# One token block ahead of the other: block 0 goes alone from attention to its first gathered rows, block 1 follows in pieces among them

## The chip, the core and the metric

The kernel runs as one program on one core of a Trainium2 chip. The core has TensorE (PE, matrix products), VectorE (DVE), ScalarE (ACT), GpSimd (POOL) and SyncE (SP), each with its own in-order instruction stream, and sixteen DMA engines that move data between the chip's memory and the core. Streams meet only at semaphores. In this kernel SP issues the weight loads, POOL issues the gathers and some loads, ACT a few. The metric is the device time of one execution in microseconds; the median of three runs of the kernel before is 1559.52 us (1557.63 to 1566.49).

## The reference

The input is 256 tokens of width 1024 in float32, one layer. The first half computes

```python
h = rms_norm(x, attn_norm_g)
q, k, v, qi, ki, wi, glu_in, gates = split(h @ w_in)
y_att = dsa_attention(q, k, v, qi, ki, wi, rel_bias) @ w_att_out   # 64 keys of 256 kept per token by an index score
y_conv = conformer_conv(glu_in, conv_w, ...)                       # depthwise, 31 taps, layer norm, silu, @ w_conv_out
g = sigmoid(gates + b_gate)
x = x + (g[0] * y_att + g[1] * y_conv) @ w_out
h2 = rms_norm(x, ffn_norm_g)
x = x + peer(h2, w_peer_q, sub_keys, expert_u, expert_v)
x = x + sigmoid(rms_norm(x) @ w_ple_gate) * (p @ w_ple_proj)
```

`peer` is the part that matters here. Each token forms 8 heads of two queries (`h2 @ w_peer_q`, 2048 columns), scores each against 128 keys, takes the best 16 of each, the best 16 of their sums, and so picks 128 of 16384 experts. For each pick it takes a row of `expert_u` and one of `expert_v` (1024 numbers each): the dot product of the token with the first, through a gelu and times a softmax gate, weighs the second in the sum. The picks differ per token, so the rows are gathered. The second half is a recurrent layer (a scan in both directions over a context and over the tokens) and a convolutional feed-forward layer; the modulation of its norms comes from the product of two condition vectors with a 1024 by 6144 matrix (`ada_w`), which needs nothing of the first half.

## The kernel before

The 256 tokens are two blocks of 128, one token per partition. Weight matrices come as tiles of up to 512 columns (2 MB) into a ring of two slots: SP (`sp_weights`, L482) issues tile i when tile i-2 has been multiplied, in the order of `weight_tiles`, and two PSUM buffers G alternate in the same way (`pe_tile`, `freed`). A product is taken as features (`pe_features`, L502: weights stationary, 256 tokens as columns) or as tokens (`pe_tokens`, L512: tokens stationary, 512 weight columns); each runs over both blocks. One product of float32 matrices counts as two instructions.

Order on TensorE: `pe_project` (norm, then glu_g, glu_a, q, k, v, qi, kiwi), `pe_attention` (index scores, four gate tiles, the convolution's mean and variance, then logits, turned probabilities and values of block 0 and of block 1), `pe_mix` (conv_out, att_out, mix_out, two tiles each), `pe_queries` (norm and queries). ScalarE runs beside in `act_first` and `act_queries`, VectorE in `dve_first` and `dve_queries`. VectorE's softmax, top keys and convolution stand in that order by hand, and `some(n)` puts n units of the ada products between them (`dve_modulation`, L1135 and L1139). There are 64 units: 16 tiles of 0.5 MB are used twice and 32 once. POOL loads these 48 tiles into four slots (L1119), each when the tile four before it is used, and its later gathers stand behind the loads in its stream.

The selection (`dve_select`) works on a quarter of the heads of one block at a time. `spread_e` and `spread_g` place picks and gates over the partitions through TensorE (L1189). POOL's `pool_rows` (L1475) then issues 256 gathers, one pick of 128 tokens each: 128 rows of 8 KB, 1.05 MB, into a ring of eight. A gather waits for its quarter's picks and for the use of the row eight before it. A group is two rows: VectorE's dot products (L1490), ScalarE's gelu and diagonal (L1496 to L1506), TensorE's sum (L1521). Block 0 has groups 0 to 63, block 1 has 64 to 127.

Other work is cut into pieces that run between the groups. `run_order` lets TensorE run piece k behind group k, and VectorE and ScalarE one group later. In `beside` stand the other seven selections (ten pieces each, one begins every eight groups), the last query tile (five pieces), the context's norm and projections (from piece 10), the scan over the context, and the ple projection: 126 places of 128 groups. Behind the last group come ple, the scan over the tokens and the feed-forward layer.

## Time and profile before

| | us |
|---|---|
| median of 3 runs | 1559.52 |
| lowest, highest run | 1557.63, 1566.49 |
| profiled execution: span from first to last instruction | 1554.9 |
| the runs' median less that span | 4.6 |
| first gathered row issued | 318.26 |
| last gathered row issued | 974.97 |

The trace is of one execution and times are counted from its first instruction. Its own time is known as that span; the runs were timed apart from it, and their median is 4.6 us longer. In rows of the trace "busy" of an engine is the time in which it executed something; the DMA share is the mean busy share of the sixteen DMA engines; the granted clock is a share of TensorE's full speed. "<-" behind an idle time names what ended it. Matrix products are pipelined, so that merged rows overlap by a tenth or two of a microsecond.

### The profile page before, as it was taken

To read this page: it belongs to the slowest core of one execution; us is meant where nothing else is said; L and a number is where in the kernel's file an instruction comes from. 1 tells how busy PE (TensorE), PEld (TensorE's weight loads), DVE (VectorE), ACT (ScalarE), POOL (GpSimd) and SP (SyncE) were. 2 spreads that over 40 slices of the span, in tenths; PEclk is the share of its full clock that TensorE was granted. 3 is DMA by queue.
4 is the path that set the end of the run, shared out by engine and by line. 5 is a ranking of instruction groups with operands and counts; after the bars stand their busy time and mean duration, and the time that the engine had idled before them with its cause. 6 is when DMAs were issued, how large, how long until landed. Compare 5 with 4: busy or idle time off the path is not lost.

```text
span 1554.9 us, 26679 instructions
## 1 busy us (share of the span) xinstructions
PE 1212.9 (78%) x11282; PEld 834.9 (54%) x11282; DVE 926.5 (60%) x2067; ACT 431.5 (28%) x1094; POOL 347.1 (22%) x315
## 2 busy tenths in 40 slices
PE   7989898894385533457856775799987888999998
PEld 6467784772153100125524452468877774888843
DVE  2887666657797988785677655321455343455512
ACT  2111420132432422543364332423243211110100
POOL 1000012034354555454455544000000000000000
PEclk9997999996597855569878996899999999999999
DMA  9551459699999999999999999624300023344432
GB/s 381 195 191 66 144 205 390 238 383 419 414 410 420 420 422 421 421 414 419 416 421 420 420 418 418 240 82 163 109 9 3 4 111 108 122 163 161 137 140 104
DMA packets 109720, 409.73 MB, mean 264 GB/s; under 512 B 8456, under 2 KB 33552, under 8 KB 76448
## 3 DMA queue, kind: packets, MB, share of 16 engines
q0 software_dynamic: 44576, 297.35, 46.5%
q1 hardware_dynamic: 63552, 106.48, 19.2%
q10 hardware_dynamic: 1472, 4.20, 1.0%
q8 instruction: 88, 1.44, 0.4%
q14 instruction: 32, 0.26, 0.0%
HBM read 405.89 MB, written 2.11 MB: 262 GB/s over the span
## 4 chain that ended last, share of the span: by engine, by line
PE 58%; DMA 22%; DVE 10%; ACT 4%; issue 3%; POOL 2%; another core or an unknown queue 0%; POOLq 0%; DVEq 0%; ACTq 0%; SPq 0%
PE psum L502 20%; DMA arena<-in_experts,arena 17%; PE psum L1942 8%; PE psum L2454 5%; PE psum L512 4%; DVE arena L1490 4%; PE psum L1521 3%; DMA arena<-in_lora_up 2%; PE psum L755 2%; PE psum L1269 2%; POOL arena L1475 2%; PE psum L2244 2%; PE psum L760 2%; DMA arena<-in_ada_wT 2%; PE psum L741 2%
## 5 line engine op out<-in xcount | busy, mean ns | idle before, releaser
L1475 POOL DMA_INDIRECT arena<-in_experts,arena x256 | 317.1, 1239 | 383.2 <-PE psum L1521 299.8
L1521 PE MATMUL psum<-arena 128*32 128x512 f32 x1024 | 185.4, 805 | 238.2 <-ACT arena L1506 231.6
L502 PE MATMUL psum<-actT,weights 128*128 128x256 f32 x1312 | 287.3, 381 | 0.0
L502 PEld LDWEIGHTS psum<-actT,weights 128*128 128x128 f32 x1312 | 250.3, 191 | 35.7 <-issue 1.5
L1521 PEld LDWEIGHTS psum<-arena 128*32 128x32 f32 x1024 | 22.7, 121 | 329.5 <-ACT arena L1506 307.3
L1490 DVE CUSTOM_DVE_ANT_0 arena<-arena 128x1024 f32<-128x1024 f32 x96 | 116.7, 1224 | 50.9 <-DMA arena<-in_experts,arena 50.1
L1490 DVE CUSTOM_DVE_ANT_0 arena<-weights,arena 128x1024 f32<-128x1024 f32 x96 | 116.6, 1223 | 37.1 <-DMA arena<-in_experts,arena 35.1
L1496 ACT ACTIVATE arena<-arena 128x2 f32<-128x2 f32 x128 | 26.1, 204 | 364.3 <-DVE arena L1490 350.4
L1942 PE MATMUL psum<-arena 64*64 64x64 f32 (+1 forms) x2816 | 89.7, 231 | 17.4 <-DVE arena L2059 7.1
L1942 PEld LDWEIGHTS psum<-arena 64*64 64x64 f32 x2816 | 84.1, 142 | 26.0 <-issue 14.6
L1490 DVE CUSTOM_DVE_ANT_0 arena<-normed,arena 128x1024 f32<-128x1024 f32 x64 | 77.2, 1225 | 22.1 <-DMA arena<-in_experts,arena 20.3
L1119 POOL DMA_DIRECT2D arena<-in_ada_wT x48 | 25.5, 531 | 229.7 <-DVE mod L1135 229.7
L2454 PE MATMUL psum<-weights,arena 128*128 128x512 f32 x176 | 75.7, 592 | 0.0
L512 PE MATMUL psum<-weights,actT 128*128 128x512 f32 x160 | 69.2, 592 | 0.0
L1506 ACT ACTIVATE arena<-const,arena 128x32 f32<-128x32 f32 x256 | 66.3, 306 | 0.0
L1501 ACT ACTIVATE arena<-arena 128x1 f32<-128x1 f32 x256 | 61.5, 287 | 12.1 <-ACT arena L1496 0.4
L2528 DVE SCALAR_TENSOR_TENSOR arena<-arena,small 128x256 f32<-128x256 f32 x154 | 61.9, 478 | 0.0
L2454 PEld LDWEIGHTS psum<-weights,arena 128*128 128x128 f32 x176 | 33.4, 190 | 41.7 <-issue 41.6
L1942 PEld LDWEIGHTS psum<-actT,arena 64*64 64x64 f32 x1152 | 39.3, 134 | 21.4 <-ACT arena L2027 12.0
L512 PEld LDWEIGHTS psum<-weights,actT 128*128 128x128 f32 x160 | 30.4, 190 | 37.8 <-issue 37.8
L1942 PE MATMUL psum<-actT,arena 64*64 64x64 f32 x1152 | 45.5, 221 | 5.7 <-issue 4.3
L675 ACT ACTIVATE normed<-xres 128x512 f32<-128x512 f32 (+1 forms) x13 | 9.0, 692 | 146.4 <-DVE xres L2544 60.3
(390 smaller groups left out, 1897.0 us busy)
## 6 DMA issues: line engine op xcount, KB each, us to landing
weights<-in_w_in SPq DMA_DIRECT2D x18, 2048.0 KB
arena<-in_ada_wT POOLq DMA_DIRECT2D x48, 512.0 KB, 6.3
weights<-in_ffn_w_up SPq DMA_DIRECT2D x22, 1024.0 KB
weights<-in_ffn_w_down SPq DMA_DIRECT2D x5, 2048.0 KB
weights<-in_w_out SPq DMA_DIRECT2D x4, 2048.0 KB
weights<-in_w_peer_q SPq DMA_DIRECT2D x4, 2048.0 KB
arena<-in_experts,arena POOLq DMA_INDIRECT x256
weights<-in_w_ple_gate SPq DMA_DIRECT2D x2, 2048.0 KB
```

What stands on the lines that cost most here:

```text
L502: mm = nc.tensor.matmul(out[:, c * T:(c + 1) * T], w[:, k, c * P:(c + 1) * P], act[:, k, :], start=(k == 0), stop=(k == kc - 1))
L512: mm = nc.tensor.matmul(out[:, b * 512:(b + 1) * 512], act[:, k, b * P:(b + 1) * P], w[:, k, :], start=(k == 0), stop=(k == kc - 1))
L741: mm = nc.tensor.matmul(chunk_bank(c)[:, b * P:(b + 1) * P], xres[:, b, c * P:(c + 1) * P], norm_diag[:, b, :], start=True, stop=True)
L755: mm = nc.tensor.matmul(out[:, 2 * i * T:(2 * i + 1) * T], w[:, k, 2 * i * P:(2 * i + 1) * P], actT[:, k, :], start=(k == 0), stop=(k == D ...
L1475: nc.gpsimd.indirect_dma_start(out=rows[:, n % RING, :], out_offset=None, in_=dram["experts"], in_offset=bass.IndirectOffsetOnAxis(ap=eidx ...
L1490: ins = nc.vector.tensor_tensor_reduce(rows[:, pos, 0:D], quad_row(b, k % QUADS), rows[:, pos, 0:D], 1.0, 0.0, ALU.mult, ALU.add, dots[:, ...
L1501: nc.scalar.activation(acts[:, g, j:j + 1], gelu[:, g, j:j + 1], ACT.Copy, scale=gate[:, b, bass.ds(t * RING + (g * GROUP + j), 1)]).then_ ...
L1506: nc.scalar.activation(diag[:, pos, :], K("ident_q"), ACT.Copy, scale=acts[:, g, j:j + 1]).then_inc(S("diag_ok"), 1)
L1521: mm = nc.tensor.matmul(SUMS[sum_part(k, i), i, :], diag[:, pos, :], rows[:, pos, D + 512 * i:D + 512 * (i + 1)], start=first, stop=last, ...
L1942: mm = nc.tensor.matmul(dst[half[c], g, at + q * n:at + (q + 1) * n], left(g, c, q), right(g, c, q), start=True, stop=True)
L2454: return nc.tensor.matmul(aux[2 * b + n], ffT[:, f, b * P:(b + 1) * P], w[:, k, 512 * n:512 * (n + 1)], start=(f == 0), stop=(f == FC - 1))
L2528: st.run(nc.vector.scalar_tensor_tensor(dst, src, w, dst, ALU.mult, ALU.add))
```

## The change

Block 0 is taken through attention, mixing, norm and two of four query tiles by itself. Block 1's attention runs between; its mixing, norm and queries become 19 pieces (`pe_follow`, `act_follow`, `dve_follow`) among the groups 0 to 18, and query tiles 2 and 3, which serve both blocks, lie among them. Tiles `att_out`, `mix_out` and `peer_q0`, `peer_q1` are loaded once per block. Products for one block have 128 columns (`pe_block_features`), or one group of 128 tokens (`pe_block_tokens`). The norm has tags n2a and n2b, one per block, each with a square of two halves, a root, a diagonal and turned chunks of 128 columns; each block's normed rows are written out apart.

In `dve_first` the ada units are spread as 16, 2, 6, 9, 11, 6, 3, then 5 ahead of the selection, and the last 6 behind it; VectorE mixes block 1's attention between the indices and the gates of the first selection. POOL fetches the condition vectors at its start, the keys and the norm's gain behind ada tile 8, and holds row 5 until all ada tiles are used, since rows 5 to 7 of the ring lie where the ada tiles were. The arena is laid out anew for this; scores go through G instead of a bank of their own. The selections begin at pieces 2, 11, 19 and so on, the context's work at piece 21 instead of 10, and the free place behind each pair of the scan is taken out.

```diff
-    for i in range(4):
+    def gate_tile(i):
         tile(f"gate{i}", part(w, 0, DC, GATE0 + 512 * i, 512))
+    def conv_tile(i):
+        tile(f"conv_out{i}", part(dram["w_conv_out"], 0, CC, 512 * i, 512))
+    gate_tile(2)
+    gate_tile(3)
+    conv_tile(0)
+    gate_tile(0)
+    gate_tile(1)
+    conv_tile(1)
+    for b in range(TB):
+        for i in range(2):
+            tile(f"att_out{i}_{b}", part(dram["w_att_out"], 0, CC, 512 * i, 512))
+        for i in range(2):
+            tile(f"mix_out{i}_{b}", part(dram["w_out"], 0, DC, 512 * i, 512))
+        if b == 0:
+            for i in range(2):
+                tile(f"peer_q{i}", part(dram["w_peer_q"], 0, DC, 512 * i, 512))
+    for i in (2, 3):
+        tile(f"peer_q{i}", part(dram["w_peer_q"], 0, DC, 512 * i, 512))
     for i in range(2):
-        tile(f"conv_out{i}", part(dram["w_conv_out"], 0, CC, 512 * i, 512))
-    for i in range(2):
-        tile(f"att_out{i}", part(dram["w_att_out"], 0, CC, 512 * i, 512))
-    for i in range(2):
-        tile(f"mix_out{i}", part(dram["w_out"], 0, DC, 512 * i, 512))
-    for i in range(4):
-        tile(f"peer_q{i}", part(dram["w_peer_q"], 0, DC, 512 * i, 512))
+        tile(f"peer_q{i}_1", part(dram["w_peer_q"], 0, DC, 512 * i, 512))
...
+        def pe_block_features(pe, name, src, chunks_of=4):
+            w, out = pe_tile(pe, name)
+            kc = w.shape[1]
+            for c in range(4):
+                for k in range(kc):
+                    mm = nc.tensor.matmul(out[:, c * P:(c + 1) * P], w[:, k, c * P:(c + 1) * P], src[:, k, :],
+                                          start=(k == 0), stop=(k == kc - 1))
+                if c == 3:
+                    mm.then_inc(S("tile_done"), 1)
+                if (c + 1) % chunks_of == 0:
+                    yield
+        def pe_block_tokens(pe, name, src, chunks_of=DC):
+            w, out = pe_tile(pe, name)
+            for k in range(DC):
+                mm = nc.tensor.matmul(out[:, 0:512], src[:, k, :], w[:, k, :], start=(k == 0), stop=(k == DC - 1))
+                if k == DC - 1:
+                    mm.then_inc(S("tile_done"), 1)
+                if (k + 1) % chunks_of == 0:
+                    yield
...
+            pe_index(0)
+            pe.wait_ge(S("rel_in"), 64)
+            pe.wait_ge(S("ix_relu"), 1)
+            for i in range(4):
+                mm = nc.tensor.matmul(aux[i], K("flip"), toepf[:, 512 * i:512 * (i + 1)], start=True, stop=True)
+            mm.then_inc(S("toep_pe"), 1)
+            pe_features(pe, "gate2", actT)
+            pe.wait_ge(S("toep_cp"), 1)
+            pe_logits(0)
+            pe_features(pe, "gate3", actT)
+            pe_probs_turned(pe, 0)
+            pe.wait_ge(S("cvT_ok"), CC)
+            pe_features(pe, "conv_out0", cvT)
+            pe_values_of(pe, 0)
             pe_features(pe, "gate0", actT)
+            pe.wait_ge(S("av_cp"), 1)
+            pe_index(1)
+            pe_features(pe, "gate1", actT)
             pe.wait_ge(S("ix_relu"), 2)
+            pe_logits(1)
+            pe_features(pe, "conv_out1", cvT)
+            for i in range(2):
+                all_of(pe_block_features(pe, f"att_out{i}_0", attT[0]))
+            pe.wait_ge(S("mix_ok"), 2)
+            all_of(pe_block_tokens(pe, "mix_out0_0", mixT[0]))
+            pe_probs_turned(pe, 1)
+            all_of(pe_block_tokens(pe, "mix_out1_0", mixT[0]))
+            pe_values_of(pe, 1)
...
+            top_keys(0)
+            some(6)
+            softmax_first(0)
+            softmax_last(0)
+            some(9)
             st.settle()
+            conv_mixed(0)
+            some(11)
+            top_keys(1)
+            softmax_first(1)
+            conv_mixed(1)
             for i in range(2):
+                st.settle()
+                dve_att_mixed(dve, 0, i)
+            softmax_last(1)
+            some(6)
+            dve_mix_add(dve, 0, 0)
+            some(3)
+            dve_mix_add(dve, 0, 1)
...
+        def dve_att_mixed(dve, b, i):
+            tile_, dst = f"att_out{i}_{b}", mixT[b][:, 4 * i:4 * i + 4, :]
+            tmp = (late_tmp if b else first_tmp)[:, i, :].rearrange("p (c t) -> p c t", c=4)
+            wait_freed(dve, f"gate{i}")
+            wait_freed(dve, f"conv_out{i}")
+            nc.vector.tensor_tensor(tmp, product(dve, tile_)[:, 0:512].rearrange("p (c t) -> p c t", c=4),
+                                    gatt[b][:, 4 * i:4 * i + 4, :], ALU.mult).then_inc(freed(tile_), 1)
+            wait_freed(dve, tile_)
+            nc.vector.tensor_tensor(dst, dst, tmp, ALU.add).then_inc(S("mix_ok"), 1)
+        def dve_mix_add(dve, b, i):
+            dst = halves_of(xres, b, i)
+            nc.vector.tensor_tensor(dst, product(dve, f"mix_out{i}_{b}")[:, 0:512], dst, ALU.add).then_inc(
+                freed(f"mix_out{i}_{b}"), 1)
...
             pool.dma_start(relb, dram["rel_bias"]).then_inc(S("rel_in"), 16)
             pool.dma_start(onehot, dram["onehot"]).then_inc(S("rel_in"), 16)
+            pool.dma_start(silu_c.rearrange("p n k -> p (n k)"), dram["cc"].partition_broadcast(P)).then_inc(S("c_in"), 16)
             pool.wait_ge(S("rel_cp"), 1)
             pool.dma_start(scratch, hbias).then_inc(S("rel_in"), 16)
             pool.wait_ge(S("rel_in"), 48)
             overlap = bass.AP(scratch.tensor, 0, [[1, P], [3 * P, AH], [1, T]])
             pool.dma_start(toepf.rearrange("p (s t) -> p s t", s=AH), overlap).then_inc(S("rel_in"), 16)
-            pool.dma_start(keysT, dram["keysT"]).then_inc(S("keys_in"), 16)
-            pool.dma_start(gbc, dram["ffn_norm_g"].partition_broadcast(P)).then_inc(S("gbc_in"), 16)
-            pool.wait_ge(S("chunk_pe"), DC)
-            pool.dma_start(silu_c.rearrange("p n k -> p (n k)"), dram["cc"].partition_broadcast(P)).then_inc(S("c_in"), 16)
             for j in range(6 * DC):
                 if j >= ADA_SLOTS:
                     pool.wait_ge(S("ada_used"), j - ADA_SLOTS + 1)
                 pool.dma_start(adaw[:, j % ADA_SLOTS, :], dram["ada_wT"][j * P:(j + 1) * P, :]).then_inc(
                     S(f"ada_in{j % ADA_SLOTS}"), 16)
+                if j == 2 * ADA_SLOTS:
+                    pool.dma_start(keysT, dram["keysT"]).then_inc(S("keys_in"), 16)
+                    pool.dma_start(gbc, dram["ffn_norm_g"].partition_broadcast(P)).then_inc(S("gbc_in"), 16)
         def dve_modulation(dve, st):
...
         def pe_queries(pe):
-            pe_norm_tile(pe, "n2", "peer_q0")
+            pe_norm_query(pe, 0, "peer_q0")
             pe.wait_ge(S("keys_in"), 16)
-            for i in range(QUARTERS - 2):
-                if i:
-                    pe_features(pe, f"peer_q{i}", actT)
-                pe_scores(pe, i)
+            pe_scores(pe, 0)
+            all_of(pe_block_features(pe, "peer_q1", actT[:, :, 0:P]))
+            pe_scores(pe, 1)
+            pe.wait_ge(S("av_cp"), TB)
+            for i in range(2):
+                all_of(pe_block_features(pe, f"att_out{i}_1", attT[1]))
             pe_spread(pe, "e", 0, FIRST["e"])
...
+            pe_spread(pe, "g", 0, FIRST["g"])
...
+        FOLLOW_PIECES = 19
+        def pe_follow(pe):
+            pe.wait_ge(S("mix_ok"), 4)
+            for i in range(2):
+                for _ in pe_block_tokens(pe, f"mix_out{i}_1", mixT[1], DC // 2):
+                    yield
+            yield
+            for c in range(DC):
+                pe_block_chunk(pe, 1, c)
+            yield
+            for k in range(DC):
+                chunk_copied(pe, BLOCK_NORM[1], k)
+            for _ in pe_features_by_chunk(pe, "peer_q2", actT):
                 yield
-            pe_scores(pe, QUARTERS - 1)
+            for c in pe_features_by_chunk(pe, "peer_q3", actT):
+                if c == 0:
+                    pe_scores(pe, 2)
+                yield
+            for n in (4, 5):
+                for c, _ in enumerate(pe_block_features(pe, QUERY_TILES[n][0], actT[:, :, P:2 * P], 2)):
+                    if c == 0:
+                        pe_scores(pe, n - 1)
+                    yield
+            pe_scores(pe, 5)
+            yield
...
+        def dve_follow(dve, st):
+            yield
+            dve_mix_add(dve, 1, 0)
+            yield
+            yield
+            dve_mix_add(dve, 1, 1)
+            dve_block_diagonal(dve, 1)
+            yield
+            yield
+            copy_block_chunks(dve, 1, 1)
+            yield
+            dve_block_row(dve, 1)
             yield
...
         def dve_queries(dve, st, mod):
+            dve_block_diagonal(dve, 0)
+            copy_block_chunks(dve, 0, 1)
+            dve.wait_ge(S("chunk_pe"), chunks_before("n2a") + DC)
+            dve.wait_ge(S("silu_c"), 2)
+            dve_block_row(dve, 0)
+            for _ in range(MODS_BEFORE_SELECT):
+                next(mod, None)
+            select = dve_select(dve, st, 0, 0)
+            for _ in range(7):
+                next(select)
+            for i in range(2):
+                dve_att_mixed(dve, 1, i)
+            all_of(select)
             for _ in mod:
                 pass
             dve.wait_ge(S("ada_used"), 6 * DC)
...
                     g, j = divmod(k, GROUP)
                     pool.wait_ge(S("row_used"), rows_ahead(former[0], t, g) + j + 1)
+                if n == 5:
+                    pool.wait_ge(S("ada_used"), 6 * DC)
                 nc.gpsimd.indirect_dma_start(
...
         def sp_ctx(sp):
-            wait_freed(sp, "mix_out1")
+            sp.wait_ge(S("mix_ok"), 4)
             act_load(sp, "lora", loraup, dram["lora_up"].rearrange("d p n -> p d n"))
             sp.wait_ge(S("sc_pe"), QUARTERS * TB)
+            sp.wait_ge(S("normed_out"), 32)
             act_load(sp, "ctx", ctok, dram["ctx"].rearrange("(b p) d -> p b d", p=P))
...
                 for j in range(TB):
-                    yield one(pe_pair, act_pair, dve_pair, 3 + SOLVE_LEVELS, d, j, rest=1)
+                    yield one(pe_pair, act_pair, dve_pair, 3 + SOLVE_LEVELS, d, j)
             yield one(pe_chain, None, dve_chain, NCH, rest=2)
-        SPREAD_BEFORE = 2
+        SPREAD_BEFORE = 3
         n_first = len(beside)
-        pieces = [[] for _ in range(SELECT_EVERY * (n_first - 1) + SELECT_PIECES)]
+        begins = [2] + [11 + SELECT_EVERY * i for i in range(n_first - 1)]
+        pieces = [[] for _ in range(begins[-1] + SELECT_PIECES)]
         for i, f in enumerate(beside):
             for k in range(f["pieces"]):
-                pieces[SELECT_EVERY * i + k].append((i, k))
+                pieces[begins[i] + k].append((i, k))
         early = [dict(act=act_ctx_norm, dve=dve_ctx_norm, pieces=1),
                  dict(pe=pe_ctx_in, act=act_ctx_in, dve=dve_ctx_in, pieces=17)]
         scan = list(scan_stages(ctx_m, "c"))
         early.append(scan.pop(0))
         early.append(dict(pe=pe_quads, act=act_quads, pieces=QUADS))
-        turn = SELECT_EVERY * (SPREAD_BEFORE - 2) + SELECT_PIECES
+        turn = begins[SPREAD_BEFORE - 2] + SELECT_PIECES
         for f in early:
             for k in range(f["pieces"]):
                 pieces[turn].append((len(beside), k))
                 turn += 1
             beside.append(f)
         assert turn <= len(pieces)
-        for k in range(QUARTERS + 1):
+        for k in range(FOLLOW_PIECES):
             pieces[k].append((len(beside), k))
-        beside.append(dict(pe=pe_late_queries, act=act_late_queries, pieces=QUARTERS + 1))
+        beside.append(dict(pe=pe_follow, act=act_follow, dve=dve_follow, pieces=FOLLOW_PIECES))
         n_first = len(beside)
         beside += scan
```

## Rows read from the trace of the kernel before

**Rows 1.** Page: the span in 40 slices; DMA busy tenths, then GB/s.

```profile
DMA  9551459699999999999999999624300023344432
GB/s 381 195 191 66 144 205 390 238 383 419 414 410 420 420 422 421 421 414 419 416 421 420 420 418 418 240 82 163 109 9 3 4 111 108 122 163 161 137 140 104
```

**Rows 2.** Windows: stretch, busy of PE, PEld, DVE, ACT, POOL; clock, DMA share, GB/s.

```profile
0.00:318.30 318.30, 281.86 (x1197) 212.93 (x1198) 214.34 (x459) 60.95 (x85) 30.04 (x60) 0.95 0.63 226
318.00:975.00 657.00, 400.48 (x4588) 211.93 (x4587) 486.40 (x1187) 249.97 (x784) 315.23 (x256) 0.75 1.01 418
990.00:1555.00 565.00, 521.51 (x5440) 405.36 (x5432) 218.44 (x410) 113.30 (x207) 0.00 (x0) 0.98 0.30 105
```

**Rows 3.** Timeline of POOL: start us, duration us, line, operation, idle before it.

```profile
318.26 1.01 POOL L1475 DMA_INDIRECT arena<-in_experts,arena  x1 [41.65 <-DVE arena L1444]
...
974.97 1.94 POOL L1475 DMA_INDIRECT arena<-in_experts,arena  x1 [0.30 <-issue]
```

**Rows 4.** Timeline of TensorE: first start, time of the merged instructions, count.

```profile
98.75 3.62 PE L802 MATMUL psum<-actT,weights 128*128 128x256 f32 x16
...
146.37 1.89 PE L837 MATMUL psum<-arena,const 128*128 128x256 f32 x8
...
148.09 13.98 PE L502 MATMUL psum<-actT,weights 128*128 128x256 f32 x64
...
165.52 1.71 PE L873 MATMUL psum<-arena 64*128 64x128 f32 x16 [1.72 <-ACT arena L943]
...
183.80 1.58 PE L864 MATMUL psum<-arena 128*64 128x128 f32 x16 [1.69 <-ACT arena L956]
...
186.05 2.96 PE L873 MATMUL psum<-arena 64*128 64x256 f32 x16 [0.68 <-ACT arena L959]
...
202.94 1.97 PE L856 MATMUL psum<-const,arena 128*128 128x128 f32 x16
...
231.46 7.17 PE L502 MATMUL psum<-arena,weights 128*128 128x256 f32 x32 [0.35 <-DMA weights<-in_w_att_out]
...
242.34 29.40 PE L512 MATMUL psum<-weights,arena 128*128 128x512 f32 x64 [3.70 <-issue]
...
278.28 2.95 PE L741 MATMUL psum<-normed,xres 128*128 128x128 f32 x12 [6.54 <-DVE normed L722]
...
298.53 2.02 PE L1260 MATMUL psum<-arena 128*128 128x128 f32 x16 [1.19 <-ACT arena L1311]
```

**Rows 5.** DMA issues by line: transfer, queue, KB of one, median us to landing.

```profile
xres<-in_x SPq DMA_DIRECT2D x1, 1024.0 KB, 5.1
```

**Rows 6.** Timeline of VectorE: the end of a softmax, and two ada units in a row.

```profile
200.60 2.29 DVE L1057 TENSOR_TENSOR arena<-arena 128x2048 f32<-128x2048 f32 x1
...
233.74 1.23 DVE L1135 CUSTOM_DVE_ANT_0 arena<-arena 128x1024 f32<-128x1024 f32 x1
...
234.89 1.22 DVE L1135 CUSTOM_DVE_ANT_0 arena<-arena 128x1024 f32<-128x1024 f32 x1
```

**Rows 7.** The line that loads the ada tiles: us from issue to landing.

```profile
DMA to landing us min/median/max: 3.7/6.3/13.2
```

**Rows 8.** Waits by line: us in total, times, longest us.

```profile
DVE arena L1135 <- DMA arena<-in_ada_wT: 11.2, 12, 2.2
```

**Rows 9.** Window of the norm and the interleaved half of the first query tile.

```profile
278.28:290.50 12.22, 12.22 (x66) 11.37 (x67) 4.43 (x8) 1.90 (x4) 0.00 (x0) 0.88 0.45 177
```

**Rows 10.** Timeline of VectorE: start and end of the first selection.

```profile
300.44 0.87 DVE L1374 MAX8 arena<-arena 128x8 f32<-128x128 f32 x4 [4.34 <-ACT arena L1316]
...
317.79 0.19 DVE L1444 CAST arena<-psum 128x32 uint32<-128x32 f32 x1 [1.31 <-PE psum L1189]
```

**Rows 11.** Chain of waits, start us and us; then the window of the first.

```profile
356.95 32.78 DMA arena<-in_lora_up
389.81 11.80 DMA arena<-in_ctx
...
356.90:389.80 32.90, 11.67 (x80) 3.32 (x72) 24.51 (x71) 9.94 (x31) 14.74 (x12) 0.59 1.02 420
```

More of the change, by code:

```diff
@@ L799, in pe_project @@
             pe_features(pe, "qi", actT)
+            pe.wait_ge(S("cv_dve"), 1)
+            for c in range(CC):
+                mm = nc.tensor.matmul(AUX[:, 0, 0:T], K("conv_mean"), ycv[:, c, :], start=(c == 0), stop=(c == CC - 1))
+            mm.then_inc(S("cv_pe"), 1)
             w, out = pe_tile(pe, "kiwi")
@@ L809, in pe_attention @@
         def pe_attention(pe):
[L811 to L814 removed]
             pe.wait_ge(S("qk_n"), 1)
[L817 removed]
+            pe.wait_ge(S("cv_dve"), 2)
             for g in range(4):
```

582 lines of the change are left out of this document (341 added, 241 removed).

## The prediction

> **What bounds the kernel now.** The page's slices come first [rows 1]: the sixteen DMA engines are full (share 9, about 420 GB/s) for seventeen slices, and half idle in the eight before. The windows give the sizes [rows 2]: up to 318.3 us they run at 0.63 and 226 GB/s, from 318 to 975 us at 1.01 and 418 GB/s, while TensorE has 400 of 657 us busy and VectorE 486. POOL's queue names the two ends [rows 3]: the first gathered row is issued at 318.26 us, the last at 974.97. So the kernel is three stretches in series: 318 us of dependent work before the first row, 657 us bounded by bytes (256 rows of 1.05 MB are 268 of some 275 MB), and 565 us behind (990 to 1555), which the change leaves alone. An earlier first row is worth its whole advance, but each byte added behind it costs 1/418 us per kB, that is 2.5 us per 1.05 MB, whatever hides its arithmetic.
>
> **The change, part by part.** *The path to the first row.* I walk it from 98.9 us, the end of the qi tile, which nothing moves on TensorE: ten more ada units before the convolution fill VectorE's idle time there, since the condition vector is fetched at POOL's start; if they end 3 us late, TensorE still has tile kiwi to hide it. Prices from [rows 4]; a tile of 64 instructions is 14.0, one of 32 is 7.2.
> - Convolution mean (1.9), kiwi (two halves of 3.6), 16 transposes (2.0), variance (1.9), index products of block 0 (1.7), their ReLU on ScalarE (1.0), flip (eight instructions of 512 columns, 0.46 each as in the mixing tile, 3.7): 98.9 to 118.3. The old wait of TensorE between 109 and 131 us mostly goes.
> - gate2, gate3 and logits (14.0+14.0+1.7) cover top keys and softmax of block 0 on VectorE; turned probabilities 1.0, conv_out0 7.2, values 1.6, gate0 14.0, index products of block 1 (3.0), gate1 14.0, logits 3.0, conv_out1 7.2: 199.0.
> - Output tiles of one block have 128 columns instead of 256. At 128 columns 16 instructions take 2.02, so 0.126 each; 32 per tile are 4.0. The first ends at 203. The second's 1 MB is issued when conv_out1 ends; 1 MB lands in 5.1 [rows 5], so it runs from about 205 to 209, and VectorE's two products and sums (1.4) end at 210.4.
> - Mixing: a token tile of one block is a quarter of the 29.40 shown for 64 instructions, 7.35. Its 2 MB (about 10 by twice 5.1) is issued at 203: it runs 213 to 220, then 16 transposes 2.0, the second mixing tile to 230.
> - VectorE has the end of block 1's softmax (two passes of 2.29 and a reciprocal [rows 6]) to 215.2, then nine ada units. Four are loaded, one every 1.15 [rows 6]. The others wait for loads: 6.3 us from issue [rows 7], then 2.0 apart (1.15, and 11.2/12 of waiting as in the old row [rows 8]). That gives 231.9, so the addition (half of a pass of 1024, 0.7) ends at 232.6: VectorE, not TensorE, is late here. Square, root, reciprocal and diagonal (0.8+0.3+0.5 and handovers): 234.5.
> - Norm and first query for one block: the interleaved half took 12.2 [rows 9] for both blocks. Half its columns, but a chain of copies that doesn't halve: 8.1 (6 to 12 possible). The remaining half of the tile 4.0. Two copies, scores and copy 2.6: 249.2. VectorE meanwhile owes five ada units, the last loaded late: 251.8.
> - Selection from the first maximum to the indices took 300.44 to 317.98, 17.5 [rows 10]: 269.3. TensorE has its first spread ready only just in time: query 1 (64 of 0.126, 8.1), its scores, and block 1's att_out (twice 4.0, the second's weights landing about 262) end near 267. The first row isn't free yet: POOL issues in order, and the load of ada tile 47 stands before the rows and waits for tile 43. VectorE first mixes block 1 (3.0), ends the selection's gates (2.0) and uses tiles 42 and 43 (2.3); POOL's issue 0.5. **First row at 277**, against 318.3: a gain of 41. Ends: 262 if the ada loads are never late and handovers cost nothing beyond the rows, 292 if each of some forty handovers costs 0.4 more.
>
> Narrow matmuls ahead of the first row: 128 instructions (two att_out tiles and the first query tile of 64). At 0.126 us [rows 4] they cost little more than half of a 256-column one (14.0/64, 0.219). The Trainium skill (TensorE: Matmul & The Clock Gate, Back-to-back issue gap) speaks against this: spacing is set by weight load and matmul together, with about 81 ns at 128 columns and 131 at 512. By that ratio one would take 0.28 here (0.62 of 29.40/64), and the 128 would cost 20 us more than by the row.
>
> *What stands behind the first row.* New inside the byte-bound stretch: query tiles 2, 0 again and 1 again (6.3 MB), the rest of tile 3, which was partly loaded before 318 (1.4), two ada tiles (1.05) and block 1's normed rows (0.5): 9.3 MB at 418 GB/s is 22. The second set of att_out and mix_out lands by about 277 (mix_out is issued at 262 and 267). Ends 18 (all weights for pieces come a tile earlier) and 27 (both mix tiles inside).
>
> POOL's new wait at row 5 for all ada tiles holds every later row, and with them all four engines. Tiles 46 and 47 are issued at 277, land by 283.5 (13.2 at the worst), and are used by 286. Rows 0 to 4 and the two tiles are 6.3 MB, 15 us of transfers, so the DMA has work to 292: nothing, at worst 4.
>
> *The pieces.* TensorE gets 19 pieces of at most 6 us among groups that the DMA brings every 5; old pieces of the same kind did not lower the DMA share. Their weights are the risk. In the old run 2.6 MB of weights took 32.78 us beside gathers [rows 11], 80 GB/s, a fifth. Up to the context's norm (piece 21) the weight queue must bring six tiles, lora and context, 14.2 MB: 177 us at that rate, from about 293. The 46 rows that go with it are 48 MB, 142 us at the other 340 GB/s. So TensorE, and VectorE at the context's norm, will wait for weights with groups queued behind. The ring's eight rows (20 us) go on meanwhile; once it is empty, weights have all engines to themselves and catch up. What is lost is each restart: a group's products (1.1), POOL's issue (1.0) and the first landing, about 3.5. I count two: 7. Ends 0 and 32 (rival 2). A gain is excluded, since the stretch already runs at 1.01.
>
> *At nothing:* block 1's additions, copies and row on VectorE (about 5 us; it has 170 idle in the stretch), the removed rests between scan pairs (125 pieces instead of 126, of 128 groups), the spread banks and the arena's new layout. If the scan no longer fitted before the last group, its remainder would show behind the rows, a few us.
>
> **Sum.** Profiled span 1554.9 - 41 + 22 + 7 = 1542.9. The runs' median 1559.52 is 4.6 above that span, so **1547**.
>
> **Rivals.**
> 1. *The ada loads are not in the way.* For it: until VectorE's last block-0 softmax they have long pauses to run ahead. Against: four slots, and the old kernel stood on them twelve times. First row at 262, 24 of bytes (mix_out not landed), 3 of restarts: -29, **1531**.
> 2. *Slower: the weight queue stays at 80 GB/s even when the rows pause.* Then 177 us of weights set the 23 groups that by bytes take 62 MB/418 = 149, and the ring idles for the rest: about 32 instead of 7, net +13, **1572**. It decides once weights get under some 95 GB/s (14.2 MB in 149 us). For it: the 32.78. Against: 1 MB landed in 5.1 with little beside it.
> 3. *A late first row:* TensorE's handovers, or a lower clock after waits, bring it to 295. Then -23 + 21 + 7, **1564**: the bytes eat the advance, no change.
> 4. *Narrow matmuls spaced by their weight loads:* twelve of 128 columns took 2.95 just after a wait, 0.246 each [rows 4]. At that price the 128 cost 15 more: **1562**. The skill's rule above says the same in kind.
>
> **How the numbers follow.** Forecast 0.50 (own range 1536 to 1558), rival 1 0.18, rival 2 0.12, rival 3 0.16, rival 4 0.04. What a measurement tells from no change is 0.5%, 7.8 us. The forecast's case gives faster 0.40 and same 0.10; rival 1 faster 0.18; rivals 3 and 4 same 0.17 and slower 0.03; rival 2 slower 0.12. Range 1522 to 1573, which takes in rival 2's price and a first row at 262 without restarts.
>
> **What would show it.** POOL's first gather near 277, released by VectorE's use of an ada tile, not by the indices; first-row advance minus rows' end advance near 29; weights in the chain of waits among groups 6 to 22, and a dip of the DMA share at two places there; the last 565 us the same. Wrong if the row stretch grows by under 15 or over 45 us, or if the first gather is past 292.

## The result

The changed kernel takes 1590.2 us (median of four runs, 1585.9 to 1592.0), the kernel before 1558.6 beside it: a ratio of 1.0195, 95% interval 1.0165 to 1.0225. It is slower by 31 us, where 1547 was forecast, and outside the range. The profiled run took 1591.4, its span 1589.6, 34.7 more than before.

The page's slices [rows 1] and the windows [rows 2] of the changed kernel:

```profile
DMA  9643958899996999999999999724300032444442
GB/s 353 231 133 122 341 180 305 278 421 421 418 405 239 419 420 421 421 420 414 419 420 421 419 418 420 312 80 159 106 9 3 4 109 71 154 149 143 141 152 105
```

```profile
0.00:307.36 307.36, 257.26 (x1202) 199.75 (x1202) 207.35 (x453) 58.94 (x90) 29.93 (x60) 0.93 0.68 240
307.36:1003.95 696.59, 427.04 (x4790) 239.49 (x4791) 495.40 (x1204) 254.07 (x791) 314.56 (x256) 0.77 0.99 406
480.00:500.00 20.00, 5.30 (x24) 1.97 (x24) 11.71 (x50) 8.28 (x18) 2.73 (x2) 0.50 0.27 89
```

A thirteenth slice of 239 GB/s is new: a hole in the stretch that was full before. POOL's timeline gives the two ends [rows 3], and the hole from POOL's side:

```profile
307.36 2.04 POOL L1771 DMA_INDIRECT arena<-in_experts,arena  x1 [0.31 <-issue]
...
465.31 0.93 POOL L1771 DMA_INDIRECT arena<-in_experts,arena  x1 [0.30 <-issue]
496.31 1.79 POOL L1771 DMA_INDIRECT arena<-in_experts,arena  x1 [30.06 <-PE psum L1817]
...
1003.95 0.93 POOL L1771 DMA_INDIRECT arena<-in_experts,arena  x1 [0.30 <-issue]
```

The first row is 10.9 earlier, not 41; the last is 29.0 later; from it to the end there are 585.6 us, before 579.9. So -10.9 + 39.9 + 5.7 = +34.7, the spans' difference.

**A ledger of the DMA.** GB/s times length gives the bytes of a window; bytes over 420 GB/s, the rate of the full stretches, give the time that they need; what is left of the time is "not full", whether the engines were idle or busy at a lower rate. Before, [rows 2] give 71.9 MB up to 318.3 and 274.6 to 975: 346.5 MB, 825 us, 150 not full (147 of them ahead of the first row). After: 73.8 + 282.8 = 356.6 MB, 849 us, 155 not full (132 ahead of the first row, 23 among the rows). The 10.1 MB more are 24 us. The time that is not full, which the change would have had to cut, even grew by 5.

**Where the first row lost 30 us.** TensorE's timeline of the changed kernel, and the walk in the prediction beside it: tile qi (84.9 before, 95.7 now), gate2 (118.3 forecast, 131.5), gate0 waits for its weights, the first att_out tile of block 0 (199.0 forecast, 217.3).

```profile
52.63 43.20 PE L551 MATMUL psum<-weights,actT 128*128 128x512 f32 x96 [6.09 <-DMA weights<-in_w_in]
95.66 13.98 PE L541 MATMUL psum<-actT,weights 128*128 128x256 f32 x64
...
131.49 13.98 PE L541 MATMUL psum<-actT,weights 128*128 128x256 f32 x64
...
174.78 15.77 PE L541 MATMUL psum<-actT,weights 128*128 128x256 f32 x64 [4.37 <-DMA weights<-in_w_in]
...
217.29 3.73 PE L935 MATMUL psum<-arena,weights 128*128 128x128 f32 x32
```

The line of tile qi in the kernel before, and the line that loads the ada tiles up to 60 us, before and after:

```profile
84.93 13.98 PE L502 MATMUL psum<-actT,weights 128*128 128x256 f32 x64
...
arena<-in_ada_wT POOLq DMA_DIRECT2D x7, 512.0 KB, 10.3
...
arena<-in_ada_wT POOLq DMA_DIRECT2D x12, 512.0 KB, 10.7
```

VectorE begins the selection at 269.7 (251.8 forecast) and has the picks at 285.7, and then waits for the spread, as its timeline shows; the chain of waits has the cause, the second att_out tile of block 1:

```profile
269.73 0.87 DVE L1668 MAX8 arena<-arena 128x8 f32<-128x128 f32 x4
...
285.45 0.29 DVE L1734 TENSOR_TENSOR arena<-arena,const 128x128 f32<-128x128 f32 x1
299.46 0.19 DVE L1738 CAST arena<-psum 128x32 uint32<-128x32 f32 x1 [13.71 <-PE psum L1410]
```

```profile
275.81 17.87 DMA weights<-in_w_att_out
293.68 0.04 issue
293.73 5.47 PE psum L935 x32
299.19 0.24 PE psum L1410 x8
```

So the 30 are 10.7 at tile qi, 7 more up to the selection, 12.5 at the spread. These are times of one execution; a3 below shows that another can differ by 7.7 here.

**The hole.** The chain of the rows' stretch [rows 11] holds the lora load and, begun only when it has landed, the context:

```profile
342.18 43.00 DMA weights<-in_w_peer_q
...
404.82 28.48 DMA weights<-in_w_peer_q
...
445.70 35.16 DMA arena<-in_lora_up
480.95 5.52 DMA arena<-in_ctx
```

The 35.16 are not the price of lora's 0.5 MB. SP had issued `ctx_v`, a weight tile of 2.1 MB, 0.4 us ahead of it on the same queue; that tile took 29.5 to land, and lora landed 6 behind it. The two are 2.6 MB in 35.2 us, 74 GB/s, near the 80 of the kernel before [rows 11]:

```profile
445.29 0.37 SPq L521 DMA_DIRECT2D weights<-in_w_in  x1
445.70 0.60 SPq L588 DMA_DIRECT2D arena<-in_lora_up  x1
...
weights<-in_w_in SPq DMA_DIRECT2D x1, 2048.0 KB, 29.5
```

The groups behind the context's norm stand until 486.5, POOL has issued its eight rows by 466, and when the last of them has landed there is next to nothing to move (share 0.27 from 480 to 500).

### The profile page after: what moved, and what is told of

It is laid out like the page before. It is cut to its first block, busy times and chain, and to the rows that moved or that the text cites. A ratio compares the mean times of both kernels' runs of the same rounds, so it can differ in the third digit from the quotient of the medians.

```text
span 1589.6 us, 27114 instructions
## 1 busy us (share of the span) xinstructions
PE 1213.9 (76%) x11474; PEld 847.8 (53%) x11474; DVE 928.6 (58%) x2076; ACT 433.8 (27%) x1112; POOL 345.4 (22%) x315
## 4 chain that ended last, share of the span: by engine, by line
PE 53%; DMA 32%; DVE 7%; ACT 4%; issue 3%; POOL 2%; SPq 0%; POOLq 0%; DVEq 0%; ACTq 0%
DMA arena<-in_experts,arena 19%; PE psum L541 17%; DMA weights<-in_w_peer_q 6%; PE psum L2239 5%; PE psum L551 5%; PE psum L2751 5%; PE psum L1817 3%; DVE arena L1786 3%; DMA weights<-in_w_in 3%; DMA arena<-in_lora_up 2%; PE psum L2541 2%; PE psum L935 2%; POOL arena L1771 2%; PE psum L947 2%; PE psum L801 1%
## 5 line engine op out<-in xcount | busy, mean ns | idle before, releaser
L1817 PE MATMUL psum<-arena 128*32 128x512 f32 x1024 | 176.5, 769 | 228.1 <-ACT arena L1802 228.0
L541 PE MATMUL psum<-actT,weights 128*128 128x256 f32 x1248 | 273.1, 381 | 4.4 <-DMA weights<-in_w_in 4.4
L541 PEld LDWEIGHTS psum<-actT,weights 128*128 128x128 f32 x1248 | 237.9, 191 | 38.5 <-DMA weights<-in_w_in 4.6
L2239 PE MATMUL psum<-arena 64*64 64x64 f32 (+1 forms) x2816 | 82.5, 223 | 17.7 <-DVE arena L2356 7.1
L2239 PEld LDWEIGHTS psum<-arena 64*64 64x64 f32 x2816 | 78.3, 135 | 24.3 <-issue 11.1
L1797 ACT ACTIVATE arena<-arena 128x1 f32<-128x1 f32 x256 | 61.4, 287 | 12.4 <-ACT arena L1792 0.7
L2825 DVE SCALAR_TENSOR_TENSOR arena<-arena,small 128x256 f32<-128x256 f32 x154 | 61.9, 480 | 0.0
L1200 DVE SCALAR_TENSOR_TENSOR arena<-arena,small 128x256 f32<-128x256 f32 x120 | 47.6, 482 | 0.0
L2239 PEld LDWEIGHTS psum<-arena,actT 64*64 64x64 f32 x896 | 39.6, 156 | 12.4 <-issue 4.5
```

What stands on the lines that cost most here:

```text
L541: mm = nc.tensor.matmul(out[:, c * T:(c + 1) * T], w[:, k, c * P:(c + 1) * P], act[:, k, :], start=(k == 0), stop=(k == kc - 1))
L1200: st.run(nc.vector.scalar_tensor_tensor(ycv[:, c, :], src, w, ycv[:, c, :], ALU.mult, ALU.add))
L1797: nc.scalar.activation(acts[:, g, j:j + 1], gelu[:, g, j:j + 1], ACT.Copy, scale=gate[:, b, bass.ds(t * RING + (g * GROUP + j), 1)]).then_ ...
L1817: mm = nc.tensor.matmul(SUMS[sum_part(k, i), i, :], diag[:, pos, :], rows[:, pos, D + 512 * i:D + 512 * (i + 1)], start=first, stop=last, ...
L2239: mm = nc.tensor.matmul(dst[half[c], g, at + q * n:at + (q + 1) * n], left(g, c, q), right(g, c, q), start=True, stop=True)
L2825: st.run(nc.vector.scalar_tensor_tensor(dst, src, w, dst, ALU.mult, ALU.add))
```

## The experiments

Times are medians of 5 to 12 runs; the ratio is to the kernel before, run between them on the same chip (1558.4 to 1559.0). a1 to a4 each alter the changed kernel in one place.

**a1_spread_first.**

```diff
+            pe_spread(pe, "e", 0, FIRST["e"])
             for i in range(2):
                 all_of(pe_block_features(pe, f"att_out{i}_1", attT[1]))
-            pe_spread(pe, "e", 0, FIRST["e"])
...
+            for _ in range(2):
+                next(mod, None)
             for i in range(2):
                 dve_att_mixed(dve, 1, i)
```

> TensorE spreads the first picks ahead of block 1's two att_out tiles, and VectorE does two of its last ada units ahead of mixing block 1, so that POOL's last two ada loads no longer stand behind them. All expectations are against the changed kernel (1590.2 us; first gather 307.4, context landed 486.5, DMA share 0.27 from 480 to 500). Both theories: first gather near 291. Theory A (an earlier first row is worth its advance less the bytes that then fall behind it; some 3.5 MB, 8 us): 1582. Theory B (the weights' order sets the row stretch: the context still lands near 486, whenever rows begin): the hole before it grows by about as much as the first row gains, 1590 within 3.

1581.7, ratio 1.0146 (1.0122 to 1.0169). First gather 286.79, 20.6 earlier; last gather 996.58, 7.4 earlier; the DMA share from 480 to 500 is 0.42, from 460 to 480 it is 0.82. Theory A's number, though the context also came earlier (issued 471.5, not 481).

**a2_quads_late.** It moves the quad tokens: eight loads, issued by ScalarE, that bring block 0's normed tokens back from the chip's memory, 256 KB into 32 partitions each.

```diff
-            for half in range(2):
-                act_quad_tokens(act, half)
             act_query(act, 1)
             act_scores(act, 1)
             for _ in act_select(act, 0, 0):
                 pass
+            for half in range(2):
+                act_quad_tokens(act, half)
```

> ScalarE issues block 0's eight quad-token loads behind the first selection instead of ahead of query 1. If the second att_out tile of block 1 landed late (17.9 us for 1 MB, DMA share 1.0 at 240 to 270 GB/s) because of these loads, it lands about 284 instead of 293.7, the first gather is near 297, and every later weight starts 10 us earlier: 1580 by theory A and by theory B. Rival (the wait is due to the ada and row-out traffic, or the tile is only issued too late): first gather within 3 of 307, time within 3 of 1590.

1580.7, ratio 1.0141 (1.0112 to 1.0171), as expected. In the chain the second att_out tile of block 1 now takes little more than half as long:

```profile
271.48 9.55 DMA weights<-in_w_att_out
```

First gather 294.35. The loads ahead of the selection were the cause of that wait: this 1 MB took 17.0 to 18.8 in the five runs with the quad tokens there (the changed kernel, a1, a3, a4, b3) and 5.5 to 9.6 in the nine that load all of it with the quad tokens later.

**a3_ctx_first.**

```diff
-        ACT_LOADS = ("lora", "ctx", "pT", "gup", "fg")
+        ACT_LOADS = ("ctx", "lora", "pT", "gup", "fg")
...
+                if name == "ctx_v":
+                    sp_ctx(sp)
                 if name == "ctx_lora":
-                    sp_ctx(sp)
+                    sp.wait_ge(S("mix_ok"), 4)
+                    act_load(sp, "lora", loraup, dram["lora_up"].rearrange("d p n -> p d n"))
...
         def sp_ctx(sp):
-            sp.wait_ge(S("mix_ok"), 4)
-            act_load(sp, "lora", loraup, dram["lora_up"].rearrange("d p n -> p d n"))
```

> SP issues the context ahead of ctx_v and of the lora load, which it stood behind. Theory A and B alike, if this order alone makes the hole: context landed near 460 instead of 486.5, no hole at 480 to 500 (DMA share 0.27 before), 13 to 15 us less: 1576. Rival (the hole is only moved, since ctx_v, 2 MB, now comes 1 MB later and TensorE waits for it with groups queued behind): 1586 to 1590, and a wait for ctx_v's weights in place of the context's.

1569.8, ratio 1.0076 (1.0054 to 1.0098): 1.2% of 1559 less than the changed kernel, 19 us, where 14 was expected. The context landed at 453.2. The window that was a hole is full:

```profile
0.00:299.67 299.67, 251.87 (x1202) 194.35 (x1202) 207.50 (x453) 59.06 (x90) 30.07 (x60) 0.95 0.69 246
299.67:981.63 681.96, 430.31 (x4792) 240.41 (x4792) 495.59 (x1204) 254.89 (x796) 318.12 (x255) 0.77 1.01 416
480.00:500.00 20.00, 16.90 (x92) 10.40 (x93) 16.87 (x51) 4.42 (x20) 8.95 (x8) 0.81 1.02 421
```

Not full among the rows: 6.5 us, 23 before the edit. The edit takes the context ahead of two loads, `ctx_v` and lora; which of them made the wait was not tried apart, but by the landings above it was mostly `ctx_v`. Up to 440 us this program is the changed kernel's; that its first gather is at 299.67 shows how far one execution differs from another there (7.7).

**a4_ada_later.** `some(16)` and `some(2)` become `some(6)` and `some(12)`.

> Ten ada units go back from ahead of the convolution to behind it (6 and 12 instead of 16 and 2), so that their loads and the keys' stand no longer beside the weights of tiles glu to q. Theory (the ada loads held up the weights, 6.1 us at tile q and 2 to 3 ahead of it): tile qi begins near 86 instead of 95.7, the first gather is 8 to 10 earlier, and so is the end: 1581. Rival (VectorE is late after the convolution and takes the same 10 us there: ten units of 1.15): qi near 86, but the first gather within 3 of 307 and the time within 3 of 1590.

1587.0, ratio 1.0181 (1.0159 to 1.0204), not told apart from the changed kernel's. TensorE's timeline has tile qi 10 earlier, and the gain given back at the transposes, which wait for VectorE:

```profile
85.67 13.98 PE L541 MATMUL psum<-actT,weights 128*128 128x256 f32 x64
...
116.43 3.30 PE L992 MATMUL psum<-const,arena 128*128 128x128 f32 x16 [8.14 <-DVE arena L1214]
```

The first gather is at 302.63, 4.7 earlier, and the time 3.2 less: a little past the rival's 3 us on both, but within what executions differ by, and far from the theory's 1581. So the rival holds: ten units cost about as much behind the convolution as their loads cost ahead of it.

**b1_three** has the edits of a1, a2 and a3. **b2_earlier** has them too, with the two ada units behind `dve_block_diagonal(dve, 0)`, and `some(10)`, `some(8)`.

> The three edits that gained by themselves, in one kernel: picks spread ahead of block 1's att_out, quad tokens behind the selection, context ahead of ctx_v and lora. Theory A (an earlier first row is worth its advance less the bytes that then fall behind it): first gather near 284 (it was 299.7 with the context's edit alone, 1569.8), last gather 7 to 9 earlier than there, so 1561. If the three gains of 8.5, 9.5 and 20 simply add: 1552. Theory B (the weight queue sets the stretch): the row stretch is as long again as the first row is early, a new hole (DMA share under 0.9 in some 20 us) at the context or the query tiles, 1568 to 1570.

> As b1_three, but the two ada units stand in VectorE's wait behind block 0's diagonal, so that POOL's last ada loads are out before the indices, and the units ahead of and behind the convolution are 10 and 8 (16 and 2 before). Theory A: first gather 5 to 8 earlier than in b1_three, near 277; each us of it worth about half after the bytes: 3 to 4 less than b1_three. Theory B: the same time as b1_three within 2.

1564.2, ratio 1.0041 (1.0018 to 1.0064), and 1564.4, ratio 1.0038 (1.0023 to 1.0052). b2's windows:

```profile
0.00:282.13 282.13, 245.19 (x1133) 187.58 (x1134) 202.21 (x441) 59.00 (x90) 29.93 (x60) 0.95 0.69 248
282.13:976.98 694.85, 440.13 (x4861) 250.38 (x4861) 499.62 (x1212) 254.09 (x791) 316.30 (x255) 0.78 1.01 413
```

The first gathers are at 286.61 and 282.13, 13 and 17.5 ahead of a3's, the last at 980.82 and 976.98, only 0.8 and 4.7 ahead. By the ledger a3 and b2 move the same bytes (357 MB); b2 has 3.3 MB more of them behind its first row. Neither theory gave 1564 for both.

**b3_fewer_bytes**, on a3; **b4_before_ctx_first**, a3's edit made in the kernel before.

```diff
+                    few = 1 if name in ("peer_q0_1", "peer_q1_1") else kc
-                    sp.dma_start(dst[:, :, at:at + n], view).then_inc(S(f"landed{i % WSLOTS}"), 16)
+                    sp.dma_start(dst[:, 0:few, at:at + n], view[:, 0:few, :]).then_inc(S(f"landed{i % WSLOTS}"), 16)
```

> The context's edit (1569.8), and of the second loads of query tiles 0 and 1 only the first of eight chunks is loaded, 3.67 MB less; the products run at full length on what the slots held, so the second block's picks differ. If bytes alone set the row stretch at 418 GB/s: 8.8 less, 1561. If TensorE's waits for these tiles hold groups up besides: 14 or more less, 1556 or under. If other work sets the pace there: 1567 or more.

> The kernel before with the context's load ahead of ctx_v and lora. If the hole belongs to the changed kernel alone (in the kernel before VectorE waited 4.5 us for the context, and the DMA share stayed at 1.0): 1559 within 3. If a late context cost the kernel before too: 5 or more less, 1554 or under.

b3: 1559.6, ratio 1.0013 (0.9999 to 1.0027), 10.2 less than a3 for 3.67 MB: 2.8 us per MB, where the full rate gives 2.4, near the forecast for bytes alone. b4: 1558.5, ratio 0.9999 (0.9988 to 1.0011): the hole is the changed kernel's own.

**c1_free_bytes** is b2 with `few` for all six second loads. **c2_spaced** is b2 with more groups for a piece's weights:

```diff
-        FOLLOW_PIECES = 19
+        FOLLOW_PIECES = 21
...
-                for c, _ in enumerate(pe_block_features(pe, QUERY_TILES[n][0], actT[:, :, P:2 * P], 2)):
+                for c, _ in enumerate(pe_block_features(pe, QUERY_TILES[n][0], actT[:, :, P:2 * P], 1 if n == 4 else 2)):
...
-                if n == 2:
+                if n in (2, 3):
```

**c3_quads_ctx** has the edits of a2 and a3.

> As b2_earlier (1564.4), but of all six second loads (block 1's att_out, mix_out, query tiles 0 and 1) only an eighth is loaded, 9.2 MB less; the products run at full length on what the slots held, so block 1's part of the output differs. Ledger theory (time to the last gather = bytes over 0.42 MB/us + time in which the DMA engines are not full): 7.3 to 9.2 MB less behind the first row, 18 to 22 us less, 1542 to 1547, so that the split alone, without its bytes, is 11 to 16 faster than the kernel before. Rival (the weights' waits or TensorE's pieces set the stretch, bytes come along for nothing): 1555 or more. Rival (both): under 1538.

> As b2_earlier (1564.4), but block 1's products with the second load of query tile 0 are four pieces in four groups instead of two pieces, so that the weights behind them have 10 us more. If TensorE's waits for these weights (share 0.89 at 420 to 440, 0.92 at 320 to 340) are worth their dip: 2 to 4 less, 1561. Rival (the context's norm, now one piece behind the last scores instead of three, waits for its load with groups queued): 3 to 10 more, 1568 to 1574.

> b1_three without the edit that spreads the picks first: quad tokens behind the selection and the context ahead (1569.8 with the context alone, 1564.2 with all three). Ledger theory: the spread moved 4 MB of weights from ahead of the first row to behind it and saved about as much idle time, so it was worth 0 to 2: 1564 to 1566. If an earlier first row is worth half its advance (13 us in b1_three): 1570 or so here.

c1: 1541.5, ratio 0.9899 (0.9877 to 0.9920), 22.9 less than b2, the upper end of the ledger's 18 to 22 within the noise.

```profile
0.00:281.56 281.56, 243.63 (x1133) 186.38 (x1134) 202.48 (x441) 59.09 (x90) 29.92 (x59) 0.95 0.67 243
281.56:958.41 676.85, 435.02 (x4863) 244.40 (x4862) 499.23 (x1213) 254.94 (x796) 318.04 (x255) 0.78 1.01 414
```

68.4 + 280.2 = 348.6 MB: 8.4 less than b2, 20 us, and 18.6 earlier at the last gather. The split is worth 17 us on the kernel before when its weights cost nothing.

c2: 1559.3, ratio 1.0009 (0.9994 to 1.0023), 5 less than b2; the share from 420 to 440 is 1.02, 0.89 in b2. c3: 1559.2, ratio 1.0007 (0.9988 to 1.0026), 5 less than b1 and under both of its forecasts, with a first gather at 291.31, 4.7 later. Beside the other two edits the spread put first looks like a loss (the intervals overlap a little): in b1 TensorE takes block 1's att_out behind it, so that the first mixing weights are issued at 289.25, in c3 at 277.98, and b1's TensorE waits 9.4 at the first mixing piece, c3's nothing. That this alone is the loss was not tried by itself. c3's windows:

```profile
0.00:291.31 291.31, 253.46 (x1202) 195.62 (x1202) 206.99 (x453) 59.13 (x90) 29.94 (x60) 0.95 0.68 246
291.31:976.01 684.70, 428.36 (x4792) 237.38 (x4792) 495.86 (x1204) 254.51 (x796) 320.86 (x256) 0.77 1.01 417
270.00:280.00 10.00, 7.03 (x58) 6.49 (x58) 9.55 (x48) 3.54 (x5) 0.00 (x0) 1.00 0.94 295
280.00:290.00 10.00, 3.68 (x45) 3.34 (x44) 7.26 (x16) 0.63 (x2) 0.53 (x1) 0.87 1.04 275
```

**d1_no_spread** is c3 with c2's pieces; **d2_units_early** adds b2's two early ada units; **d3_spaced_more** gives the last query tile four groups as well (23 pieces); **d4_rows_held** is c3 with one wait in POOL:

```diff
+                if n == 0:
+                    i_ = tile_at["mix_out1_1"]
+                    pool.wait_ge(S(f"landed{i_ % WSLOTS}"), landed_at[i_])
```

> c3_quads_ctx (1559.2) with the spaced pieces of c2: no early spread. If the spacing's 5 us (b2_earlier to c2_spaced) come from TensorE's wait for query weights, which c3_quads_ctx has too (12.9 us, share 0.92 at 420 to 440): 1554 to 1556, under the kernel before. Rival (c3 has taken the same idle time out already): 1559 within 2.

> d1_no_spread with two ada units in VectorE's wait behind block 0's diagonal, so that POOL's last ada loads are out before the indices: first gather 4 to 5 earlier, with the weights' order as in d1. Theory W (rows that start before block 1's mixing weights have landed only slow these down: they land in 8 us ahead of rows, in 22 to 31 beside them): within 2 of d1_no_spread. Theory A (half the advance): 2 to 3 less.

> d2_units_early with the second load of query tile 1 spread over four groups too, and the context's work two pieces later. If TensorE still waits for that tile's weights in d2: 1 to 3 less than d2. If only one wait had been left: the same within 2.

> c3_quads_ctx (1559.2; first gather 291.3), but POOL holds the first gather until block 1's second mixing tile has landed. Theory W: the mixing weights land in about 8 to 12 us each instead of 22, the first gather is some 8 later (about 299), and the time is the same within 3. Theory A (an earlier first row is worth half its advance): 1563 to 1565. Full worth: 1567.

d4: 1570.7, ratio 1.0090 (1.0073 to 1.0106), 11.5 more than c3. POOL's timeline shows the hold, 11.74, and the window what it left empty:

```profile
284.95 0.53 POOL L1345 DMA_DIRECT2D arena<-in_ada_wT  x1 [0.62 <-DVE mod L1364]
297.23 1.01 POOL L1777 DMA_INDIRECT arena<-in_experts,arena  x1 [11.74 <-DMA weights<-in_w_out]
```

```profile
290.00:300.00 10.00, 0.00 (x0) 0.00 (x0) 3.16 (x10) 0.00 (x0) 2.17 (x3) 0.50 0.66 244
```

Theory W falls. By the medians theory A's half looks too small as well: the hold and the loss are nearly equal, as if the first row were worth its whole advance where nothing else is put behind it. The traces do not show that. From first to last gathered row d4 takes 678.5 us and c3 684.7, so 6.2 of the hold come back among the rows. But d4's profiled execution is its fastest (1565.7), c3's lies 4 above its median, and against d1, which holds nothing either, the loss is 7.8. Whole or half stays open.

d1: 1562.9, ratio 1.0034 (1.0017 to 1.0050); d2: 1560.8, ratio 1.0015 (1.0001 to 1.0030); d3: 1560.3, ratio 1.0013 (1.0001 to 1.0024). The spacing, 5 us beside the early spread, is worth nothing measurable without it (c3 to d1, where 1554 to 1559 was expected). d2's first gather is at 279.13, and it gains 2.2 on d1, theory A's 2 to 3, but the intervals overlap. b3, c2, c3, d2 and d3 are all within 0.3% of the kernel before, d2 and d3 just above it by their intervals. Only c1, which leaves out seven eighths of the second loads, is faster; none of these kernels beats it with its whole work done.

## Why the prediction was wrong

**First row at 277: failed by 30, the largest error in the sum.** It was not what cost the most time: a1 took 20.6 of it back and gained 8.5 us, while the hole was worth 19 (a3). The walk began "from 98.9 us, the end of the qi tile, which nothing moves on TensorE". The ada units moved ahead take their loads with them, beside the weights of the tiles up to q: up to 60 us the changed kernel loads twelve ada tiles, where the kernel before loaded seven, and TensorE waits 6.1 for tile q. Yet a4 shows that undoing this is worth no measurable time, since VectorE owes the units elsewhere. The second miss is block 1's att_out: "the second's weights landing about 262", the products to end "near 267", when they ended at 299.1. I priced it at TensorE's 4.0 per tile and at a landing of 5 to 6, and left out who else loads there: the quad tokens, which [rows 5] could not show. It took 17.9, and 9.55 without them beside it (a2). The products took 5.5 per tile, not 4.0, at a mean granted clock of 0.68 and 0.69: the first tile's began behind a wait of 7.1 and ran 2.3 us at 0.50, the lower of the two levels (1.2 GHz). The last link, "released by VectorE's use of an ada tile, not by the indices", held (POOL's last ada load went out at 306.52), but the spread set when VectorE came to that tile.

**22 for bytes: right in size, by luck.** 282.8 less 274.6 MB is 8.2, 20 us, but with a first row at 307. With one at 282, near the forecast's 277, block 1's mixing weights fall behind it and the bytes are 12.4 MB, 30 us (b2). b3 gives 2.8 us per MB for a part of them and c1 22.9 us for 9.2.

**Two restarts of 3.5, 7: should have been 20.** The place was named (the context's norm, weights with groups queued behind), the price was not. I took it that "once it is empty, weights have all engines to themselves and catch up". They do: the context alone lands in 5.5. But what the groups waited for was two loads in series. The first of them, lora, was begun while the rows were still full on, behind the 2.1 MB of `ctx_v` in its own queue (35.2 for the two), and the context was not issued before it had landed. The ring's eight rows ran out meanwhile. Nothing in the work needs `ctx_v` or lora first; a3 turned the order and got 19 back. Rival 2 came nearest: the queue at a fifth of the rate, 177 us for six tiles, lora and context from 293 on, which is 470; the context landed at 486.5. Its price for this term, 32, was too high, and its 1572 had a first row at 277. Two things in it were not so: when the rows pause, the queue is fast (5.5 for the context), and the slow rate itself is no bound once the order is mended (in a3 a query tile of 2.1 MB still took 28.6, 73 GB/s, and the stretch was full).

The weight queue had the share that its packets give it. From 405 to 430 us, with the engines full (share 1.02), the changed kernel's gathers (q0) and weights (q1) moved nearly the same number of packets:

```profile
q0 software_dynamic: 1124, 8.19, 78.3%
q1 hardware_dynamic: 1109, 2.24, 23.2%
```

A packet of the weights is 2.0 kB there and one of the gathers 7.3 kB, so one for one the weights get 0.21 of the bytes, 90 GB/s. The chain's 28.48 us for 2.1 MB, from issue to landing, are 74 GB/s. The Trainium skill (DMA: Bandwidth & Descriptors, Queues, rings and completion order) says that an engine takes a packet from each queue in turn. The equal counts agree, though the skill's packet holds several descriptors and no run shows that the profile counts the same unit.

**565 us behind the rows "the same": about 4 off.** From the end of the last row's product to the end of the program are 563.2 us before and 567.5 after; 564 to 570 in the experiments. No cause was found, and none was tried.

**Narrow matmuls:** [rows 4] were right, 32 of 128 columns took 3.73 (0.117 each) and rival 4 fell; block 1's took 5.5 (0.17 each), and 3.73 over their clock of 0.68 is 5.5. The Trainium skill's ratio (TensorE: Matmul & The Clock Gate, Back-to-back issue gap), 0.28 here, did not hold.

**What the sum missed as a whole.** An advance of the first row counts only as far as the DMA engines were not full in it and are afterwards. In b2 the first row is 36 earlier than before, close to the 41 forecast, and the time 6 longer: 12.4 MB more lie behind the first row, not 9.3 (30 us), 8 us more are not full among the rows, and the stretch behind them is 5 longer (584.9): -36 + 30 + 8 + 5 = +7. From 270 to 290 us the engines were busy without rows, at 0.94 to 1.04 (c3's windows): what a row takes from there comes back behind it. In d4 the rows wait while the engines stand partly idle (share 0.66), and there the loss is 7.8 to 11.5 us for a hold of 11.7. What these kernels win at the first row is not enough for the weights loaded twice: with seven eighths of those left out, c1 is 17 us faster than the kernel before.

## What to carry to other kernels

When a stretch is bound by bytes, keep a ledger over the stretches together: bytes over the full rate, plus the time in which the engines are not full; an edit gains only what it takes off one of the two, and a second load of a matrix is paid in full. Before you move a load, write down the queue that it stands in and what else is in flight then: 1 MB landed in 5.5, 9.6 or 17.9 us, and 0.5 MB in 35 behind 2.1 MB of its own queue. And let no load wait for another on a queue that gets a fifth of the rate, if the work behind it holds up the rows.

## What the runs showed of the hardware

Block 0's quad tokens, eight loads of 256 KB into 32 partitions each, kept the DMA engines busy at a low rate: share 1.04 at 275 GB/s from 280 to 290 us in c3 (window above), where a full stretch moves 420. In that window two queues moved bytes, the quad tokens' (q10) and the weights' (q1):

```profile
q10 hardware_dynamic: 384, 1.23, 53.4%
q1 hardware_dynamic: 741, 1.52, 50.2%
```

That is 230 GB/s of the engines' time for the quad tokens and 303 for the weights beside them; beside the gathers, from 405 to 430 in the changed kernel, the weights moved at 386 of theirs (2.24 MB in 23.2% of 25 us). A busy share of 1 is not yet the full rate, and another queue gets less beside such loads: with them 1 MB of weights took 17.9, with them later 9.55.
